# Order of the output products in a chunked delta-rule recurrence

## The reference, cut to what matters

```
def step(S, xs):
    qd, kd, ui, wi, ai, gl = xs
    v_new = ui - jnp.einsum('bhck,bhkv->bhcv', wi, S)
    o = jnp.einsum('bhck,bhkv->bhcv', qd, S) + jnp.einsum('bhcs,bhsv->bhcv', ai, v_new)
    S = S * jnp.exp(gl)[..., None, None] + jnp.einsum('bhck,bhcv->bhkv', kd, v_new)
    return S, o
```

## Time and profile before

| | us |
|---|---|
| median of 3 runs | 3531.97 |
| lowest and highest | 3530.44, 3535.03 |
| profiled execution, its own time | 3535.0 |
| its span | 3533.1 |
| PE busy | 3450.6 |
| DVE busy | 2779.7 |
| ACT busy | 1571.4 |
| mixer of layer 0, from its first set-up to its last sums | about 200 to 375 of the span |
| mixer of layer 1, likewise | about 1950 to 2126 |

### The profile page before, as it was taken

The page is one execution under the profiler, slowest core; times in us unless marked ns, Lnnn a source line. Parts: engine busy times, 40 slices in busy tenths (PEclk is TensorE's granted clock), DMA queues, the critical chain, the costliest instruction groups (busy, mean ns, idle before and its releaser), DMA issues.

```text
span 3533.1 us, 59685 instructions
## 1 busy us (share of the span) xinstructions
PE 3450.6 (98%) x19944; PEld 3254.5 (92%) x19944; DVE 2779.7 (79%) x5688; ACT 1571.4 (44%) x2511; POOL 1151.3 (33%) x860
## 2 busy tenths in 40 slices
PE   8999999999999999999999899999999999999998
PEld 6877799999999999999988778999999989999997
DVE  7357588898997888888773666888889978888886
ACT  5344433336785333333443444333377753333333
POOL 0000012227775345444100000122177753554450
PEclk9999999999999999999999999999999999999999
DMA  4200244458999999999432002444589999999992
GB/s 148 80 19 1 68 140 145 144 166 289 345 336 358 344 368 388 377 381 380 163 102 78 7 1 78 147 150 148 173 320 337 343 356 355 379 380 376 386 365 95
DMA packets 266843, 814.19 MB, mean 230 GB/s; under 512 B 24880, under 2 KB 107056, under 8 KB 263088
## 3 DMA queue, kind: packets, MB, share of 16 engines
q1 hardware_dynamic: 93168, 339.06, 26.7%
q0 software_dynamic: 73728, 268.47, 20.7%
q10 hardware_dynamic: 99776, 204.50, 16.2%
HBM read 709.17 MB, written 102.76 MB: 230 GB/s over the span
## 4 chain that ended last, share of the span: by engine, by line
PE 89%; DVE 4%; DMA 3%; ACT 1%; issue 1%; POOL 0%; ACTq 0%; DVEq 0%; SPq 0%
PE bank L455 25%; PE bank L456 25%; PE bank L457 25%; PE bank L1509 5%; PE bank L1275 2%; DMA gath<-slabs,rows_of 1%; DMA gath<-u_rows,rows_of 1%; PE bank L514 1%; PE bank L490 1%; PE bank L1465 1%; PE bank L1376 1%; PE bank L1375 1%; DMA hidden_dram<-hst 1%; PE bank L1204 1%; PE bank L1187 0%
## 5 line engine op out<-in xcount | busy, mean ns | idle before, releaser
L452 DVE TENSOR_TENSOR wlo<-raw,whi 128x1024 fp32r<-128x1024 f32 x628 | 794.8, 1266 | 406.8 <-ACT whi L406 377.0
L455 PE MATMUL bank<-act_hi,whi 128*128 128x384 f32 (+1 forms) x2848 | 1010.3, 355 | 6.3 <-ACT hst L931 3.3
L456 PE MATMUL bank<-act_lo,whi 128*128 128x384 f32 (+1 forms) x2848 | 998.5, 351 | 0.0
L457 PE MATMUL bank<-act_hi,wlo 128*128 128x384 f32 (+1 forms) x2848 | 998.2, 351 | 0.0
L406 ACT ACTIVATE whi<-raw 128x1024 fp32r<-128x1024 f32 x628 | 665.9, 1061 | 722.5 <-PE bank L457 703.0
L455 PE MATMUL bank<-w_hi,whi 128*128 128x384 f32 x2048 | 685.5, 335 | 2.6 <-DVE w_lo L2161 2.6
L457 PE MATMUL bank<-w_hi,wlo 128*128 128x384 f32 x2048 | 684.1, 334 | 0.0
L456 PE MATMUL bank<-w_lo,whi 128*128 128x384 f32 x2048 | 684.1, 334 | 0.0
L622 POOL TENSOR_TENSOR onehot<-onehot,cidx 128x800 f32<-128x800 f32 x56 | 123.9, 2244 | 1443.1 <-DVEq L2035 1443.1
L455 PEld LDWEIGHTS bank<-act_hi,whi 128*128 128x128 f32 x2848 | 537.1, 189 | 39.0 <-ACT hst L931 3.6
L635 POOL DMA_INDIRECT gath<-slabs,rows_of x256 | 436.4, 1705 | 403.7 <-DVE acc L2196 355.7
(11 more groups left out here) (322 smaller groups left out, 3917.9 us busy)
## 6 DMA issues: line engine op xcount, KB each, us to landing
raw<-slabs SPq DMA_DIRECT2D x636, 512.0 KB, 4.8
hidden_dram<-hst ACTq DMA_DIRECT2D x256, 192.0 KB, 4.0
gates_dram<-stage ACTq DMA_DIRECT2D x24, 2048.0 KB, 7.5
h_sb<-hidden_dram ACTq DMA_DIRECT2D x64, 768.0 KB, 8.2
g_sb<-gates_dram ACTq DMA_DIRECT2D x32, 1536.0 KB, 18.8
gath<-u_rows,rows_of POOLq DMA_INDIRECT x256, 7.9
gath<-slabs,rows_of POOLq DMA_INDIRECT x256, 9.1
res<-x_t SPq DMA_DIRECT2D x2, 1024.0 KB, 7.1
```

Of the source, the lines that this page charges most:

```text
L452: nc.vector.tensor_tensor(wlo[k][:], raw[k][:], whi[k][:].bitcast(F32), ALU.subtract).then_inc(s_slab_lo, 1)
L455: nc.tensor.matmul(out, a_hi, b_hi, start=first, stop=False)
L456: nc.tensor.matmul(out, a_hi, b_lo, start=False, stop=False)
L457: return nc.tensor.matmul(out, a_lo, b_hi, start=False, stop=last)
```

## The change

For a chunk, the kernel before issues for head 0 the product with the state and then the one with the new values, then the same for heads 1, 2 and 3. Each head is an accumulation group of its own (start on the first, stop on the second). The changed kernel issues the four products with the state first, then the four with the new values. Only the very first has the start flag and only the very last the stop flag. The operands, the shapes, the number of matmuls and all waits and signals are the same.

```diff
@@ -1371,10 +1371,12 @@
                         if c > 0:
                             pe.wait_ge(S["og_copied"], c)
                         for hd in range(H):
-                            out = bank[3][:, hd * CHUNK:(hd + 1) * CHUNK]
-                            nc.tensor.matmul(out, state[c % 2][:, hd, :], qdec[t % 2][:, hd, rows], start=True, stop=False)
-                            last = nc.tensor.matmul(out, vnew[rows, hd, :], intra[t % 2][rows, hd, rows],
-                                                    start=False, stop=True)
+                            nc.tensor.matmul(bank[3][:, hd * CHUNK:(hd + 1) * CHUNK], state[c % 2][:, hd, :],
+                                             qdec[t % 2][:, hd, rows], start=hd == 0, stop=False)
+                        for hd in range(H):
+                            last = nc.tensor.matmul(bank[3][:, hd * CHUNK:(hd + 1) * CHUNK], vnew[rows, hd, :],
+                                                    intra[t % 2][rows, hd, rows], start=False,
+                                                    stop=hd == H - 1)
                         last.then_inc(S["step_o"], 1)
```

## The result

The changed kernel took 3501.01 us (median of 4 runs, 3497.78 to 3507.07), the kernel before 3531.2 (median of 4, 3527.38 to 3535.03). The ratio is 0.9905, with a 95% interval from 0.9889 to 0.9922: 30.2 us faster. A second set of runs gave 3502.13 against 3532.19 (ratio 0.9917, 0.9899 to 0.9935), a third 3506.26 against 3533.22 (0.9921, 0.9903 to 0.9939).

The account below looks back on a forecast made before the run. PE, busy 98% of the span, was taken to bound the kernel. 12.9 us from removed changes at full clock plus 7 from the clock made about 20: 3535.0 - 20 = 3515 us, range 3507 to 3523.

Parts of the forecast that it names:

- The price of a change of kind: In the mixer's outputs, switching between 128*128 and 64*128 loads costs 0.1425 us; 6 fewer per output save 0.855 us.
- At half clock the price: In output B of tile 2, a change of kind costs 0.28 us, 0.14 more than at full clock.
- case B: Mixer: the changes go, the clock falls as now; 12.9 + 1.5 = 14.4 us gained, 3519 to 3521; chance 33%.
- The flags at nothing: In the outputs, start and stop flags ride on matmuls that are there anyway and cost nothing.
- DVE stays behind PE: In tiles 0 to 2, DVE's idle time before line 1827 falls from 1.96 to 1.1 us, still waiting for PE.
- The last tile gives less than 1.71 us: Last tile: PE waits for the final attention weights, gaining 1.3 to 1.4 us; 0.8 comes off over two layers.
- The clock: Mixer's half-clock stretches: between 0 beyond the 1.5 and 13.0 us come back; 6 to 7 us taken.
- case C: Mixer: the clock no longer falls there; 3535.0 - 25.9 = 3509 us; chance 17%.
- A: Outputs: loads cannot run beside a matmul of the same rows; about 2 us saved, 3530, no change; chance 6%.
- D: Mixer: PE reaches its waits sooner, the clock falls in every tile; 9 us slower, 3541; chance 3%.

Follow-up runs that it names:

- two by two: Old order changed to heads 0 and 1 both products, then heads 2 and 3, against the kernel before: 3512.92 us against 3531.14, ratio 0.9961.
- the dummies: Changed kernel plus 48 tiny pairs of a 64-row and a 128-row matmul: in the inverse 3519.01 us, at the end of the outputs 3528.37.
- the flags alone: Kernel before in its old order, with one start and one stop flag for the bank: 3530.85 us against 3531.14, ratio 0.9996.
- the changed kernel again: The changed kernel run once more without any edit, against the kernel before: 3502.13 us against 3532.19, ratio 0.9917.
- the kernel with the dummies in the inverse: Changed kernel plus 48 tiny pairs of a 64-row and a 128-row matmul in the dense matrix inverse: 3519.01 us, ratio to before 0.9964.
- the all-rows kernel: Kernel before in its old order, new-values product over all 128 rows, output A waiting for the second chunk's new values: 3513.05 us against 3531.14.

## Why the prediction was wrong

By its own steps:

- The price of a change of kind, 0.1425 us, the same 0.855 us for each output, and no cost between weights of one kind: right. The tile takes 36.10 us where 36.1 was written down, two by two gives 36.65, the dummies 0.14 to 0.15 a change. At half clock the price was read too high, 0.28 us: it took the step of a pair at its inner 0.17 us, but line 1363, which has no change, starts its loads 0.21 apart at half clock ((1.78 - 0.33) / 7, tile 2 of the kernel before, row below), so a change costs 0.61 - 2 x 0.21 = 0.19 there. The 1.5 us of case B should have been 0.5; the forecast does not hang on it.

```profile
323.75 1.78 PEld L1363 LDWEIGHTS bank<-u_sb,kdec 64*128 64x128 f32 x8 [0.23 <-issue]
```

- The flags at nothing: right, 3530.85 against 3531.14.
- DVE stays behind PE with 1.1 us of idle time: right, 1.12.
- The last tile gives less than 1.71 us because PE comes to wait for the attention weights: right. At full clock the old first mixer is 221.2 us. That comes from two executions of the old order: 228.5 us with 17.1 of half clock and 232.8 with 27.3, so 0.42 us for each us at half clock; two of the second mixers below give 0.44 ((237.9 - 231.9) / (23.9 - 10.2)). With 0.43, 228.5 - 0.43 x 17.1 = 221.2. The new one is 214.8. The difference of 6.4 us is what the sum says for a layer, 12.9 / 2 = 6.45. The second mixer gives the same within half a microsecond: 234.9, 231.9 and 237.9 us with 17.1, 10.2 and 23.9 of half clock give 227.5 at full clock by the same 0.43, 6.2 over the new 221.3.
- The clock: this step failed, as the prediction put it, "I take a point near the middle, 6 to 7 us", between nothing and 13.0. All of it came back, the prediction's case C, which it gave 17%. From the first output of a mixer to its end the old order has 10 to 24 us at half clock in each of six mixers, and the new order none in the twelve mixers that the profiles show. In the two profiles compared above, C's sum comes out to 0.1 us: 25.9 forecast, 463.4 - 437.6 = 25.8 in the mixers.
- How much the half clock cost the old order on average: the three first mixers in the old order average 229.9 us, 8.7 over their 221.2, and the three second ones 234.9, 7.4 over their 227.5. That is 16 us, where the prediction had 13.0 from one execution. It had left out the fifth stretch, 3.4 us or 1.5 us of time, which the order of the products doesn't touch. The new order keeps 1 us of the 16, and that is of the same sort, ahead of the first output. So about 15 us came from the clock, where 6 to 7 were taken.
- Why the middle was the wrong choice: tile 1 of layer 0 was taken as a sign that the kernel is close to an edge, and that was right, as two by two shows; but then the shorter output should have been taken to be off the edge, not on it. That is a reading after the result; the rows before held nothing that settled it.
- The range's low end, 3507, was set from case C at 3509 with little under it. C was counted from the profiled execution, 3535.0, and its 3 us over the median were taken for one more fall of the clock. They weren't: the mixers of that execution, 463.4 us, are no longer than the average of the old ones, 464.8. From the median of 3531.97 C gives 3506, already under the range. With the averages of the profiles, 12.6 + 15 = about 28 us in the mixers, it is 3504.
- The rest outside the mixers: of the 7.5 us in the two profiles compared, 6.6 lie between the two mixers (1521.7 us before, 1515.1 after). In nine other profiles of both orders this stretch takes 1516.8 to 1519.4, with 1518.4 for the flags alone and 1519.1 for the changed kernel again, and in the kernel with the dummies in the inverse, which has the new order, it takes 1521.5. So most of the 7.5 looks like scatter between two executions. One part of it is a wait of PE for ACT's line 931: 3.3 us in the kernel before, absent in the changed kernel's first and third profile and 2.7 us in its second. By the medians 30.2 us are measured and about 28 accounted for; whether the changed kernel gains the other 2 us outside the mixers for a reason stays open.
- The rivals: A (no change, because a load cannot run beside a matmul of the same rows) is refuted by the run of eight loads at 0.11 us with 64 columns each, the same as line 1363 has with 128: if load and matmul took turns, the two would differ. The prediction's own figures for A were too high: it took the 128 columns of line 1363 to stream in 0.110 us. Matmuls of 512 columns start 0.22 to 0.23 us apart at full clock (lines 1187 and 455 to 457), so 128 columns take about 0.06, an estimate, and A's rule would give line 1363 about 0.17 and not 0.22. That is still not the 0.11 measured. D (the clock falls more, because PE comes sooner to its waits) is refuted by 0 to 3.4 us of half clock in the new mixers; a fall behind a wait exists, though, in the last tile of the all-rows kernel.

## What to carry to other kernels

Where two products of different contraction height feed the same bank, issue all of one kind and then all of the other, with one start for the bank: each change avoided gives its price (0.14 us here) and the flags cost nothing. Look at the granted clock right behind stretches in which PE is busy by the profile but does little, and count what falls there as part of the price: here it was as large as the direct gain, and only several executions show how much of it there is, since it falls in other places each time. When the question is whether an effect that comes and goes will be gone after a change, price the case that it goes wholly as carefully as the middle. If there is a choice, make such changes beside dense work (the dummies cost about 8 us less there), and don't buy a missing change with a wait.

## What the runs showed of the hardware that was not expected

- A matmul pair of one column by one column with its two changes of kind takes no longer than the changes, 0.28 us for a dummy of four passes (6.7 us for the 24 of a mixer); the passes themselves were expected at 0.03 to 0.05 us each.
- A microsecond at half clock costs 0.43 us in this mixer, nearly the 0.5 of a stretch that PE alone bounds, although DVE and ACT are on the chain of waits for part of each tile.
- The clock fell in stretches before which the profile shows PE busy without a gap (4.00 of the 4 us ahead of 249.1), full of changes of kind, as well as behind waits (2.19 of 4 us ahead of 1955.8).
- Going to the next head, to another weight, or onto a column of PSUM written by the matmul just before costs nothing that the trace shows (0.22 us a pair in all cases). A change of the used rows costs 0.14 us.
